# The order of transfers on SyncE's queue where the down-projection of a hybrid block begins

## The reference

```
h = rms_norm(x, g_pre_ffn)
u = causal_depthwise_conv(h @ w_up, ffn_conv_w) + ffn_conv_b      # w_up: 1024 x 5632
gate, val = jnp.split(u, 2, axis=-1)                              # 2816 channels each
y = (jax.nn.gelu(gate, approximate=True) * val) @ w_down          # w_down: 2816 x 1024
return x + rms_norm(y, g_post_ffn)
```

## Time and profile before

| | us |
|---|---|
| median of three runs | 1250.87 (1247.88 to 1253.44) |
| the profiled execution, its own time | 1252.86 |
| its span, first to last instruction | 1251.0 |
| PE busy | 1175.9 (94%) |
| DVE busy | 803.3 (64%) |
| ACT busy | 537.2 (43%) |
| POOL busy | 389.8 (31%) |
| mean granted TensorE clock | 0.984 of full |

### The profile page before, as it was taken

One profiled execution on the slowest core, in us unless ns is written; L12 is line 12 of the kernel. 1 busy time (PEld: TensorE's weight loads), 2 busy tenths in 40 slices (PEclk: granted clock), 3 DMA queues, 4 the chain that ended last, 5 costly groups with the idle time before them and its releaser, 6 DMA issues.

```text
span 1251.0 us, 16935 instructions
## 1 busy us (share of the span) xinstructions
PE 1175.9 (94%) x5964; PEld 989.0 (79%) x5964; DVE 803.3 (64%) x1123; ACT 537.2 (43%) x972; POOL 389.8 (31%) x352
## 2 busy tenths in 40 slices
PE   6999999998999999994899999999999988999996
PEld 5888888887889888873788888777877776888885
DVE  6332354658777666749677877876687776464547
ACT  5211243556344554335434444534444434453451
POOL 1222000212133333113455667456654731000000
PEclk9999999999899999997899999999999999999999
DMA  7321143455333332220235353544536466986513
GB/s 271 115 96 71 57 125 93 147 143 191 97 114 96 112 89 68 75 94 23 93 144 188 115 202 132 172 159 144 169 134 202 136 235 245 394 313 192 186 49 134
DMA packets 117716, 181.85 MB, mean 145 GB/s; under 512 B 20463, under 2 KB 78607, under 8 KB 113423
## 3 DMA queue, kind: packets, MB, share of 16 engines
q1 hardware_dynamic: 117647, 180.94, 42.9%
HBM read 123.21 MB, written 57.70 MB: 145 GB/s over the span
## 4 chain that ended last, share of the span: by engine, by line
PE 22%; DVE 10%; POOL 10%; DMA 5%; issue 3%; ACT 3%; SPq 1%; POOLq 0%; ACTq 0%; DVEq 0%
DMA conv<-in_w_down 4%; POOL f_conv L2770 3%; POOL conv L2770 3%; DVE f_conv L2580 3%; POOL f_w_raw L2766 3%; PE f_ps_up L2878 3%; PE f_ps_up L2879 3%; PE f_ps_up L2880 3%; DVE f_w L2551 2%; PE sums L2812 2%; PE sums L2814 2%; PE sums L2813 2%; PE sums L2880 2%; PE sums L2879 2%; PE sums L2878 2%
## 5 line engine op out<-in xcount | busy, mean ns | idle before, releaser
L2766 POOL TENSOR_TENSOR f_w_raw<-stage 128x512 f32<-128x512 f32 x44 | 68.5, 1557 | 112.9 <-PE f_ps_up L2814 107.4
L2551 DVE TENSOR_TENSOR f_w<-f_w_raw,f_w 128x512 fp32r<-128x512 f32 (+1 forms) x55 | 65.3, 1206 | 42.8 <-POOL f_w_raw L2766 42.8
L2770 POOL TENSOR_TENSOR conv<-conv 128x512 f32<-128x512 f32 x44 | 63.5, 1443 | 58.3 <-DMA conv<-in_w_down 55.7
L2770 POOL TENSOR_TENSOR f_conv<-f_conv 128x512 f32<-128x512 f32 x44 | 66.0, 1500 | 37.1 <-DMA y_blocks<-f_conv 33.7
L207 PE MATMUL sums<-split,slab_w 128*128 128x512 f32 x192 | 75.9, 395 | 0.5 <-PEq L258 0.5
L209 PE MATMUL sums<-split,slab_w 128*128 128x512 f32 x192 | 74.9, 390 | 0.0
L208 PE MATMUL sums<-split,slab_w 128*128 128x512 f32 x192 | 74.8, 389 | 0.0
L2369 ACT CAST f_w<-f_w_raw 128x512 fp32r<-128x512 f32 (+1 forms) x55 | 43.6, 795 | 67.8 <-POOL f_w_raw L2766 67.7
L2812 PE MATMUL f_ps_up<-split,f_w 128*128 128x512 f32 x176 | 69.1, 393 | 2.1 <-DVEq L2547 1.7
L228 DVE SCALAR_TENSOR_TENSOR conv<-sums,conv_taps,conv 128x1023 f32<-128x1023 f32 (+6 forms) x39 | 46.8, 1199 | 37.4 <-ACT conv L219 36.4
L2580 DVE SCALAR_TENSOR_TENSOR f_conv<-f_ps_up,f_taps,f_conv 128x1023 f32<-128x1023 f32 (+1 forms) x44 | 56.3, 1279 | 20.5 <-ACT f_conv L2437 19.7
(11 more groups left out here) (392 smaller groups left out, 3465.1 us busy)
## 6 DMA issues: line engine op xcount, KB each, us to landing
stage<-in_w_up SPq DMA_DIRECT2D x22, 1024.0 KB, 5.7
y_blocks<-f_conv SPq DMA_DIRECT2D x22, 1024.0 KB, 5.1
conv<-in_w_down SPq DMA_DIRECT2D x11, 1024.0 KB, 7.9
w_down_sums<-conv SPq DMA_DIRECT2D x11, 1024.0 KB, 10.5
stage<-y_blocks SPq DMA_DIRECT2D x40, 256.0 KB, 5.0
f_rest_raw<-y_blocks SPq DMA_DIRECT2D x37, 256.0 KB, 5.3
x_tile<-in_x SPq DMA_DIRECT2D x12, 512.0 KB, 4.2
stage<-in_w_in SPq DMA_DIRECT2D x6, 1024.0 KB, 6.6
```

The lines of the kernel that those rows point to most:

```text
L2551: dve.tensor_tensor(out, src, hi.bitcast(F32), ALU.subtract).then_inc(s_lo[name], 1)
L2766: pool.tensor_tensor(raw_sum(m), a, b, op).then_inc(s_add[m], 1)
L2770: pool.tensor_tensor(view(out), view(a), view(b), op).then_inc(signal, 1)
```

## The change

In the last round of the loop over groups (g = 10) the loads of blocks 0 and 1 are issued between `store_y(9)` and `store_y_sums(9)`. In the loop over slots `store_y(10)` stands before slot 10 instead of slot 8. Before slot 19 stand only the sums' store, the gain and the waits; the eight loads of the residual stand one each before slots 30, 34, ..., 58. No operation on data is added or taken away, and no wait of `load_block` is changed.

```
--- before.py
+++ after.py
@@ -2257,6 +2257,7 @@
         s_bin = [sem(f"f_bin{n}") for n in range(RING)]
         s_bdone, s_bsum = sem("f_bdone"), sem("f_bsum")
         LAST, H_PARTS = 2, 8
+        RES_FROM = RING + 2 * FG
 
         def ring(s):
             n = s % RING
@@ -2314,15 +2315,6 @@
             def store_y_sums(g):
                 sp.wait_ge(s_ysum, 4 * (g + 1))
                 sp.dma_start(ys[g, 1].rearrange("p n s -> p (n s)"), conv[:, 2:4].rearrange("p c s -> p (c s)")).then_inc(s_yout, 16)
-
-            for g in range(FG):
-                load_up(2 * g + 2)
-                load_down(g)
-                if g > 0:
-                    store_y(g - 1)
-                    store_y_sums(g - 1)
-                load_up(2 * g + 3)
-                store_down(g)
 
             def load_block(s):
                 j, g = divmod(s, FG)
@@ -2345,18 +2337,30 @@
                     src = wt[g, :, source[1]]
                 sp.dma_start(ring(s)[:, HALF:D], src).then_inc(s_bin[s % RING], 16)
 
-            for s in range(SLOTS):
-                if s == RING:
+            for g in range(FG):
+                load_up(2 * g + 2)
+                load_down(g)
+                if g > 0:
+                    store_y(g - 1)
+                    if g == FG - 1:
+                        load_block(0)
+                        load_block(1)
+                    store_y_sums(g - 1)
+                load_up(2 * g + 3)
+                store_down(g)
+
+            for s in range(2, SLOTS):
+                if s == FG - 1:
                     store_y(FG - 1)
                 if s == RING + FG:
                     store_y_sums(FG - 1)
                     sp.wait_ge(s_dout, 16 * FG)
                     sp.dma_start(gain, io["g_post_ffn"][0:1, :].broadcast_to([P, D])).then_inc(s_small, 16)
                     sp.wait_ge(s_done[M_A22], UP)
-                    for t in range(T):
-                        if t == 7:
-                            sp.wait_ge(s_c21, UP)
-                        sp.dma_start(res_tile(t), io["res"][t]).then_inc(s_din, 16)
+                    sp.wait_ge(s_c21, UP)
+                if RES_FROM <= s < RES_FROM + 4 * T and (s - RES_FROM) % 4 == 0:
+                    t = (s - RES_FROM) // 4
+                    sp.dma_start(res_tile(t), io["res"][t]).then_inc(s_din, 16)
                 load_block(s)
             for t in range(T):
                 sp.wait_ge(s_row, t + 2)
```

## The result

| | before | changed |
|---|---|---|
| median of 17 runs each (lowest to highest) | 1245.84 us (1241.05 to 1253.44) | 1237.5 us (1234.12 to 1244.44) |
| ratio | | 0.9933, 95% interval 0.9914 to 0.9952 |
| the profiled execution, its own time | 1252.86 | 1239.99 |
| its span | 1251.0 | 1238.2 |
| PE busy | 1175.9 (94%) | 1170.5 (95%) |

The change gains 8.3 us (6 to 10.7 by the interval). The two profiles differ by 12.8 us of span, of which only 9.4 lie in the stage. The other 3.4 us lie ahead of it and are there already at the store of y(9) (998.33 against 1001.78), in code that is the same in both, so they are no effect of the change. "The stage" as in the last row is therefore what the experiments are compared by.

What follows compares the result with a forecast made beforehand. PE was taken to bound the down-projection, with time to win only in its two holes. -3.0 - 6.45 + 0.1 + 1.8 = -7.55 us from the median 1250.87 gave 1243.3 us, range 1240.5 to 1248.5.

Steps and rivals of the forecast that it cites:

- +1.8 for block 10: Slot 10: block 10, issued behind the last y's store, comes late and leaves PE a hole of 1.3 to 2.2 us.
- the +0.1: Blocks 2 and 3 follow the stores; the conv chain runs 2.75 us earlier, almost no slack at slot 5: 0.1 us lost.
- First hole, -3.0: PE's wait for block 0 at slot 0 closes when blocks 0 and 1 go ahead of the stores: 3.0 us gained.
- Second hole, -6.45: PE's wait at slot 8, behind the last y's store, closes: 5.0 us of waiting and 1.45 of lower clock gained.
- The residual, nothing: Eight residual loads spread behind slots 30 to 58 cost PE nothing, covered by 26% spare DMA time.
- take over the wait: Rival at slot 10: block 10 lands as late as before, only 3.1 us gained, 1247.7 us; chance 0.22.
- The conv chain's wait: Rival: late blocks 2 and 3 delay the conv start, slot 5 waits 2.6 us, 1245.9 us; chance 0.12.
- The spread residual: Rival, slots 30 to 58: full DMA engines make each of eight loads cost PE 1.35 us, 1254.1 us; chance 0.03.

Runs made afterwards that it cites:

- the part alone: Kernel before with only blocks 0 and 1 moved ahead of the stores of sums; stage 225.6 us, ratio to before 0.9975 (0.9947 to 1.0003).
- a neighbouring order: Changed kernel with blocks 0 and 1 between the stores of y's sums and of w_down's sums; stage 224.1 us, ratio 0.9945 (0.9917 to 0.9972).

## Why the prediction was right or wrong

**The size and the sign.** Forecast -7.55 us against the profiled execution, -0.6%; measured -8.3 us (0.67%), in the stage 9.4 us between the two profiles. The time itself, 1237.5 us, lies 3 us under the range, whose lower end was 1240.5. The step that failed is the last one, the reference point and its scatter: I set the gain off from the median of three runs, 1250.87, with 1 us for "the scatter of medians". The median of 17 is 1245.84, 5 us lower, and the three runs themselves spread over 5.6 us. With the right starting point the forecast would have been 1245.84 - 7.55 = 1238.3, 0.8 us from the measured time; so 5.0 of the 5.8 us between 1243.3 and 1237.5 are the reference point. The second step that failed is a term of the sum, +1.8 for block 10, which measured 0 (below). With the +0.1 it makes up the 1.9 us between the forecast 7.55 and the 9.4 in the two profiles' stages. That the timed gain came so near the forecast is partly luck: 9.45 us was the loss of one execution, and 8.5 that of another, so two terms were off in opposite directions. By its own terms the range would also run from 1240.8 to 1248.9, not from 1240.5 to 1248.5.

**First hole, -3.0.** Right: gone, and shown by the part alone, whose stage is 3.1 to 4.0 us shorter than before. The DMA engines took blocks 0 and 1 at no cost to PE; both are split by 1015.8, 2.4 us before PE needs the first. They did delay somebody: POOL, released by the store of y(9), starts 5.1 us after its issue (1003.40 against 998.33) and sat idle for 0.56 us. Its sums still end 8.8 us ahead of PE's last up-projection matmul, as before.

**Blocks 2 and 3, +0.1.** Right, and better than thought: block 2 is cast 0.1 us after PE's start of slot 0, the conv start comes 2.36 us after it, and low 5 is ready at 1029.95 + 1.22 = 1031.17 where PE wants it at 1018.20 + 13.62 = 1031.82. That this chain can pass on a delay is shown by the 2.22 us at slot 5 when blocks 2 and 3 came late.

**Second hole, -6.45.** Right in place and cause. Its size was that of one execution: 4.84, 3.56, 2.10 and 2.27 us were seen in four profiles with the store at slot 8. About 1.4 us of half rate came either here or at slot 0, and about 1 us hung on whether POOL's sum or DVE's low part of block 8 started first.

**Block 10, +1.8.** Wrong: 0. The early end of my ready time was 28.6 us after PE's start of slot 0 (1050.2 against 1021.62), and it was ready at 26.9. The low part took 1.30 us in place of 2.24, because the cast ended only as POOL's sums were nearly done (1038.62 + 5.39 = 1044.01), where I had added up POOL's old 6.18 us and DVE's old 2.24: 0.9 us. The store went out 16.4 us after slot 0 in place of 16.9, since the conv chain ran ahead of my figure: 0.5 us. The second load landed 3.8 us after its issue (1038.91 to 1042.71), where I had taken 4.0 to 4.85: 0.2 us. The store's landing was as I had it, 3.95 us (1034.60; block 10's first load is issued at 1038.55) in 3.9 to 5.0. The late ends of these intervals came from rows in which blocks 8 and 9 shared the queue. In both profiles the margin was 0.3 us, and with block 9 in the way it was gone, so the mechanism (no slack at block 10) holds and its size was off.

The rule of shared ports that the prediction cites from the Trainium skill (SBUF — State Buffer, "Who interferes with whom") agrees with the trace: where a low part of DVE starts while one of POOL's sums runs, it ends about 1.1 us after the sum does, with 0.08 and 0.23 us more than its 1.22 for block 10 in the two profiles, and about 1 us more in the profiles with a hole at slot 8. The 2.24 us of the prediction are the mean of two such parts (2.26 and 2.30).

**The residual, nothing.** Right for the changed order, and with PE on time a hole of 3.33 to 3.99 us with half rate behind it if it stays in bulk. The slack of 1.6 us that I gave the old order was that of one execution: in the other profile of the kernel before block 19 came 0.68 us late.

**The rivals.** Block 10 did not take over the wait. The conv chain's wait did not arise in the changed kernel, but did in a neighbouring order. The spread residual was never in PE's way, though the DMA engines were full until 1100.

## What to carry to other kernels

When PE catches up with its loads at a change of stage, look at every large transfer that stands ahead of the first blocks in the one queue, and move it to where the engines idle or the loads run far ahead. Closing one hole only pays if the next late thing behind it is moved too: here the later store was worth nothing alone, because the hole just moved to slot 19, and moving the residual gained nothing that could be timed until the holes ahead of it were closed. Give a range for the level of a time from the spread of the runs, and one for the gain apart from it.

## What the runs showed of the hardware that was not expected

**Behind holes of about 3 us the clock fell in some executions and not in others.** In this stage full clock went on after holes of 2.71 and 2.95 us (and after all shorter ones), and fell to 1.2 GHz after holes of 2.85, 3.08, 3.33, 3.56, 3.99 and 4.84 us. Behind the two of 3.56 and 4.84 us the first matmul was slow already; behind the others half rate began up to 1.4 us after the restart. Each time six to eight matmuls were slow, nearly all at about 0.63 us, with 1.4 to 1.6 us lost.

**Two instructions of DVE and POOL that meet take turns.** A low part of DVE takes 1.22 us alone and 2.14 to 2.31 when a sum of POOL has started just ahead of it; a sum takes 1.27 us alone and 2.14 to 2.37 the other way round. A start 0.1 us earlier or later so moves the end of a wait by 1 us.

**Where stores hand over to loads, the DMA engines move a third to two thirds of their usual rate** for two to four us (170 to 268 GB/s against 418 at about the same share, and 131 for a microsecond in the kernel before). So the place of a load among stores can cost more than its bytes. That it is the mixing alone is not shown: with only loads in flight the changed kernel has 274 GB/s at a full share for a microsecond.

```profile
1021.00:1022.00 1.00, 1.00 (x6) 0.84 (x5) 1.00 (x2) 0.76 (x1) 0.00 (x0) 1.00 1.00 274
```

**Most of the scatter between these profiles lies ahead of the stage.** In the two profiles of the changed kernel and the one with the bulk at slot 41 the stage is within 0.15 us of 220.2, while over all profiles PE's last up-projection matmul starts anywhere from 1011.05 to 1021.90 us. One visible part of that is a hole early in the up-projection, long in the changed kernel's first profile and short in the one with the bulk at slot 41:

```profile
600.11 0.80 PE L2816 MATMUL sums<-split,f_w 128*128 128x512 f32 x1 [3.60 <-DVE f_w L2555]
```

```profile
597.91 0.50 PE L2816 MATMUL sums<-split,f_w 128*128 128x512 f32 x1 [0.76 <-DVE f_w L2555]
```

This was not followed further.
